# Two pairs of expert weights in SBUF instead of three, and the third pair loaded from the first pair's products on

## What is computed

```python
def hier_moe(u, wg, bg, we, be, w1, w3, w2):
    xf = u.reshape(N, D)                              # N = 1024 tokens, D = 1024
    g_logits = xf @ wg + bg                           # 8 groups
    e_logits = (xf @ we + be).reshape(N, 8, 8)        # 8 experts in each group
    g_sel = argmax(g_logits)
    gate, expert_id = top 2 experts of the chosen group
    ...
    def expert_block(args):
        xb, e = args
        h = jax.nn.silu(xb @ w1[e]) * (xb @ w3[e])    # 1024 -> 256, 64 experts
        return h @ w2[e]                              # 256 -> 1024
    y_pad = lax.map(expert_block, (x_pad, block_e))
    y = segment_sum(y_pad * w_buf, tok_buf)
```

## Time and profile before

| | |
|---|---|
| median of 3 runs | 3600.62 us (3600.61 to 3602.58) |
| the profiled execution | 3585.2 us, its span 3583.3 us |
| TensorE busy | 3124.6 us (87% of the span), 19758 matmuls |
| VectorE, ScalarE, GpSimd busy | 1539.7, 889.9, 473.4 us |
| granted TensorE clock, mean | 0.926 of full speed |
| read from and written to HBM | 461.52 MB, 120.22 MB |

### The profile page before, as it was taken

One profiled execution on the slowest core, in us unless ns is written; L12 is line 12 of the kernel. 1 busy time (PEld: TensorE's weight loads), 2 busy tenths in 40 slices (PEclk: granted clock), 3 DMA queues, 4 the chain that ended last, 5 costly groups with the idle time before them and its releaser, 6 DMA issues. The chain is left out here.

```text
span 3583.3 us, 47692 instructions
## 1 busy us (share of the span) xinstructions
PE 3124.6 (87%) x19758; PEld 2314.4 (65%) x19758; DVE 1539.7 (43%) x2049; ACT 889.9 (25%) x1250; POOL 473.4 (13%) x468
## 2 busy tenths in 40 slices
PE   7999889968999997987699997698879996888786
PEld 6777578856788886766577885566658873333232
DVE  6656335442644444232644454466653423111113
ACT  4333322231211112121333331133343211100000
POOL 2211012210200000000200001243301000111110
PEclk9999679989999998998799999789999997999997
DMA  3332321223222224342422124512026438999998
GB/s 121 119 129 95 113 86 50 74 99 136 87 70 76 70 70 158 142 165 87 164 83 83 71 94 152 182 69 72 37 92 211 172 119 321 423 425 423 424 394 343
DMA packets 148254, 564.52 MB, mean 158 GB/s; under 512 B 20608, under 2 KB 53056, under 8 KB 126952
## 3 DMA queue, kind: packets, MB, share of 16 engines
q1 hardware_dynamic: 103264, 425.74, 31.3%
q0 software_dynamic: 39824, 125.38, 9.3%
q10 hardware_dynamic: 4984, 10.77, 0.8%
HBM read 461.52 MB, written 120.22 MB: 162 GB/s over the span
## 5 line engine op out<-in xcount | busy, mean ns | idle before, releaser
L53 PE MATMUL in_acc<-in_x_hi,in_w_hi 128*128 128x512 f32 x1024 | 411.6, 402 | 43.5 <-DVE in_x_lo L1521 39.6
L55 PE MATMUL in_acc<-in_x_hi,in_w_lo 128*128 128x512 f32 x1024 | 402.3, 393 | 0.0
L54 PE MATMUL in_acc<-in_x_lo,in_w_hi 128*128 128x512 f32 x1024 | 402.2, 393 | 0.0
L53 PE MATMUL up_acc<-up_x_hi,up_w_hi 128*128 128x512 f32 x704 | 275.7, 392 | 16.7 <-DVE up_x_lo L268 14.9
L54 PE MATMUL up_acc<-up_x_lo,up_w_hi 128*128 128x512 f32 x704 | 275.1, 391 | 0.0
L55 PE MATMUL up_acc<-up_x_hi,up_w_lo 128*128 128x512 f32 x704 | 275.0, 391 | 0.0
L53 PEld LDWEIGHTS in_acc<-in_x_hi,in_w_hi 128*128 128x128 f32 x1024 | 194.5, 190 | 94.3 <-issue 48.9
L54 PEld LDWEIGHTS in_acc<-in_x_lo,in_w_hi 128*128 128x128 f32 x1024 | 194.6, 190 | 44.7 <-issue 4.8
L55 PEld LDWEIGHTS in_acc<-in_x_hi,in_w_lo 128*128 128x128 f32 x1024 | 194.3, 190 | 41.1
L53 PE MATMUL down_acc<-down_x_hi,down_w_hi 128*128 128x512 f32 x352 | 140.9, 400 | 40.7 <-DVE down_x_lo L271 30.3
L1453 ACT CAST in_w_hi<-in_w_raw 128x1024 fp32r<-128x1024 f32 x64 | 66.9, 1046 | 399.0 <-PE in_acc L55 373.8
(11 more groups left out here) (608 smaller groups left out, 6120.4 us busy)
## 6 DMA issues: line engine op xcount, KB each, us to landing
wide_b_lo<-in_w SPq DMA_DIRECT2D x24, 2048.0 KB, 40.0
wide_a_lo<-in_ew SPq DMA_DIRECT2D x48, 1024.0 KB, 38.8
wide_a_hi<-in_w SPq DMA_DIRECT2D x24, 2048.0 KB, 35.2
wide_b_hi<-in_w SPq DMA_DIRECT2D x20, 2048.0 KB, 34.6
in_w_raw<-in_w_in SPq DMA_DIRECT2D x64, 512.0 KB, 3.3
up_w_raw<-in_w_up SPq DMA_DIRECT2D x44, 512.0 KB, 3.8
down_w_raw<-in_w_down SPq DMA_DIRECT2D x16, 1408.0 KB, 7.8
wide_w<-in_ew SPq DMA_DIRECT2D x20, 1024.0 KB, 37.9
```

Of the source, the lines that this page charges most:

```text
L53: pe.matmul(out, w_hi, x_hi, start=first, stop=False)
L54: pe.matmul(out, w_hi, x_lo, start=False, stop=False)
L55: return pe.matmul(out, w_lo, x_hi, start=False, stop=last)
```

## The change

`GROUPS` becomes 2, so there are four slots of each sort. `wa` no longer lies over wide_b_hi, `wb` no longer over wide_w; the buffers themselves stay. At the end of `merge_stage` SP loads pairs 0 and 1 and no more, and its waits for the transposes and for the squares go (the wait for `h1_stored` stays, ahead of the wait for the ids). In `expert_stage` the loop begins with pair 2, loaded when pair 0's ap (then yp) is done. `KEPT_USES`, the number of earlier uses of groups 0 and 1 that the surplus loop counts with, goes from 11 to 16.

```diff
-GROUPS = 3
+GROUPS = 2
...
             sp.wait_ge(acc_ready, 2 * NT)
-            for e, first in ((0, False), (1, False), (2, True), (3, True), (2, False), (3, False), (4, False), (5, False)):
+            for e, first in ((0, False), (1, False), (2, True), (3, True), (2, False), (3, False)):
                 weights(e, first)
-            sp.wait_ge(tr_ready, DT)
             sp.wait_ge(h1_stored, 16 * DT)
-            sp.wait_ge(sq_ready, DT)
-            weights(4, True)
-            weights(5, True)
             sp.wait_ge(ids_ready, 2)
             sp.dma_start(table, ids[:, :, :]).then_inc(ids_kept, 16)
...
-        wa = [wide[n][:, u * 4096:(u + 1) * 4096] for n in ("b_lo", "a_hi", "b_hi") for u in range(2)]
-        wb = [wide["a_lo"][:, u * 2048:(u + 1) * 2048] for u in range(4)] + [wide["w"][:, u * 2048:(u + 1) * 2048] for u in range(2)]
+        wa = [wide[n][:, u * 4096:(u + 1) * 4096] for n in ("b_lo", "a_hi") for u in range(2)]
+        wb = [wide["a_lo"][:, u * 2048:(u + 1) * 2048] for u in range(4)]
```

## The result

| | before | changed |
|---|---|---|
| median, 7 runs each | 3602.58 us (3600.61 to 3606.80) | 3613.56 us (3608.06 to 3617.99) |
| ratio of the two | | 1.0038, 95% interval 1.0023 to 1.0054 |
| the two timed again, 35 and 12 runs | 3602.15 us | 3612.15 us, ratio 1.0025 (1.0011 to 1.0040) |
| the profiled execution, its span | 3585.2, 3583.3 us | 3608.06, 3606.5 us |

The change makes the kernel 0.1 to 0.5% slower, by the two intervals together: 11 us in the first measurement, 10 in the second.

The account below looks back on a forecast made before the run. It took the end to be set by when the unpausing weight stream starts and the bytes left then. +14.9 - 4.1 = +10.8 us on the profiled 3585.2 gave 3596.0, plus 15.4 to the median: 3611.4 us, range 3603 to 3620.

Parts of the forecast that it names:

- Step 1: Expert stage's weight stream: one pair fewer prefetched, so 32 pairs to bring instead of 31, +14.9 us.
- Step 2: Router: without 4.2 MB beside it the last token store lands sooner and PE starts earlier, -4.1 us.
- The remark that the ranks would not move: Router: the ranks DVE waits for meet the same traffic ahead of them, costed at nothing.
- Step 3: Expert stage's stream: slots for two pairs instead of three cost nothing; landing time falls to about 24 us.
- Steps 4 and 5: Stream's start, where pair 3 waits 1 to 2 us, and tail (h1, outputs, final sum): no added cost.
- a shorter router: Rival, router: ranks come one store step, 4.7 us, earlier, leaving +6.1 us, 3606.7; chance 0.15.
- The shallower stream: Rival, expert stage: the two-pair stream starves at times, 0.5 us x 30 pairs = 15 us, 3626; chance 0.12.
- become faster: Rival, expert stage: the shallow stream saves 0.8 us on each of 28 pairs, -12 us in all, 3589; chance 0.04.
- The third pair: Rival, prefetch: its early load is worth nothing, only the 4.1 us gain remains, 3596.5; chance 0.02.

Follow-up runs that it names:

- e4: Changed kernel with only pair 0 prefetched, pair 1 too loaded after pair 0's products: 3616.34 us, ratio to before 1.0038.
- e5: Kernel before, six slots, only pair 2's first projections moved from the router to the expert stage's start: 3599.44 us, ratio 0.9990.
- e2: Kernel before, six slots kept, pair 2 not prefetched but loaded when pair 0's products have ended: 3609.68 us, ratio 1.0026.
- e8: Kernel before, six slots, pair 1 and pair 2's second projections after two token stores, pair 2's first ones at expert stage's start: 3591.03 us, ratio 0.9976.
- e9: As e8, but pair 1's second projections load at once and pair 2's second ones after all eight token stores: 3593.48 us, ratio to before 0.9978.
- e3: Kernel before, six slots, pair 2 loaded without a wait at the expert stage's start, not in the router: 3599.40 us, ratio 0.9993.

## Why the prediction was right, point by point

**Step 1, one pair more for the stream: +14.9 us.** From the refill to pair 33 it took 14.8 us more, 525.7 against 510.9, and e4's second missing pair 15.3. The estimate rested on weights at 423 GB/s without the indirect transfers, and the lower end of its bounds was the nearer one. The 17.6 us that the Trainium skill's limit of 358 GB/s would give ("DMA: Bandwidth & Descriptors", Specifications, where it is a stack's bandwidth divided by two cores) came in neither run. Here one core runs alone.

**Step 2, the router: -4.1 us.** The measured gain up to the refill is 3.3 us against the first profile of before, 1.9 against the second; to PE's start it is 3.8 and 2.1. The order of events was right: the last token store now lands in 2.6 us, where I had expected 3 to 6, and the gather follows the token list. One part of what is missing in the 4.1 is the first products of pair 0, 9.4 us in place of 8.9, the next is the list itself, 0.4 us later. Against the second profile of before the step comes to half of its size and falls under its lower bound of 3 us, because the store that it removes from the chain had landed 1.7 us sooner after the burst there (issued 0.4 sooner, 1.2 less to landing). So the step was sized too large. That this wait varies from execution to execution could not be read from one profile. e5 shows that the cause was named rightly: the 4.2 MB alone.

The remark that the ranks would not move held: 29.2 and 29.0 us against 28.8 and 30.1. e4 shows why it had to be argued: with most of the front of the burst gone they come 11 us earlier.

**Step 3, the depth: 0.** Period 16.54 against 16.51 us, landing in 21 to 24 us as forecast (24), and e2 settles it. The 38 to 40 us of before in the prediction are those of two of the tiles; wide_a_hi and wide_b_hi had 35 (the page of before), which changes nothing in the argument.

**Steps 4 and 5.** Pair 3 waited 1.34 us in the changed kernel, expected 1 to 2. The tail was costed at nothing; it is 1.1 us shorter, 0.9 between the second profiles. In size this is the time of the last pair's products, 7.09 us against 8.40 in the earlier trace rows; in the profiles of both kernels they take 7.1 us after every wait of up to 1.8 us in the stream and mostly 8.4 to 10 after longer ones. That the one causes the other was not tested.

**The sum.** +10.8 forecast, +10.4 between the first profiles, +11.0 and +10.0 between the medians. That it comes out within half a microsecond is in part luck: 0.8 us too much was put on the router and 1.1 us of the tail was left out, and these two misses nearly cancel. The second profiles differ by 644.4 - 632.1 = 12.3 us. The absolute number, 3611.4, lies 2.2 under the measured 3613.56. 2.0 of these are the median of before, which four more runs moved from 3600.62 to 3602.58. Two ends in the range have no working: the 17.5 us for the pair lie above the step's own bound of 16.5 and no run shows them (14.8 and 15.3), and a shorter router with a gain of 5 us gives 3605.8, not 3603.

**The rivals.** The shallower stream did not starve; the share of 0.67 in the earlier trace rows belongs to the moment at which the depth falls from three pairs to two. e2 has it too, 0.69 from 3502 to 3517 us, and the changed kernel, whose depth does not fall, has 1.01 there; both need 525.7 us, so the dip costs nothing. Whether single engines had run ahead in it was not looked at. It did not become faster: with two groups all along the period is 16.54 us and only the last two pairs take 15.64 and 15.51, as they did before (15.56 and 15.81), so it is not the depth that makes them quick. The router did not become shorter beyond the one wait. The third pair was worth its whole transfer. The rule to double-buffer (the Trainium skill, "Trainium Kernel Development and Optimization", Best Practices) holds for the steady stream, as e2 shows, and does not speak of its start, where the third pair counted.

## What to carry to other kernels

Where a stream of transfers bounds the end, two things set the time: when it may start for good, and how many bytes are left then. A further buffer is worth the bytes that it lets you move while the DMA engines are idle, at the stream's rate, and nothing for its depth once the queue does not run dry (here with two pairs of slots as with three). And small stores on a critical path should not be issued beside a bulk prefetch: hold back the part of it that they would meet, as e8 does, and ask of each new place which store or gather it meets there. e9 shows that a finer placing need not gain more.

## What the runs showed that was not expected

A 512 KB store that shares the DMA engines with a burst of weights lands up to 14 us after its issue (13.98 in the earlier trace rows, 14.02 and 7.99 in e8), alone after 2.6 (the last ones of the changed kernel). The order in which the same 14.7 MB of weights are issued around the router is worth 7 to 10 us from the burst to the end (e8 against before: 625.3 and 623.4 against 633.5 and 632.1) and 11 us by both pairs of medians, about as much as the whole change costs.

The time of one and the same kernel moves by over 20 us between executions (3586.24 to 3609.90 in 26 runs of before). The three profiles shown part between 300 and 600 us, where the granted clock was 0.83 in one of them and 0.77 or 0.78 in two. That is not all of it: in e3, with 0.77 there as well, the burst comes at 2974.26 us, 11.7 later than in the changed kernel. What decides the clock, and what else moves the time, was not tried.
